# HGRN rounds of a hybrid decoder layer: scores in three groups between products, the first a round ahead, sample dots beside the head squares

## The chip, the cores and the metric

The kernel runs on one core of a Trainium2 chip. The metric is the device time of one execution in microseconds, the median of several runs. Beside it stands one profiled execution, from which all rows come. Round numbers in this text count from 0.

## The reference, cut to what matters

One layer (DEPTH = 1) for a prompt of 512 tokens and a sample group of 8 single tokens that share the weights. The part that the change touches is branch A, the HGRN2 recurrence (8 heads, state 64x64), and the projections that run beside it:

```python
u = xn @ w_in                       # xn: RMSNorm(h), 1024 wide; all branches' columns in one product
f = lb + (1 - lb) * sigmoid(hf)
# HGRN2, chunk by chunk; q = silu(hq), k = 1 - f, v = hi
cum = cumsum(log(f))                                  # within a chunk
o_inter = (q * exp(cum)) @ s
scores[t, s_] = sum_k q[t, k] * exp(cum[t, k] - cum[s_, k]) * k[s_, k]    # s_ <= t
o = o_inter + scores @ v
s_new = exp(last) * s + (k * exp(last - cum)).T @ v
a_hg = head_rmsnorm(o) * silu(hg)
# the 8 sample tokens: one step S = f * S0 + k v^T, o = S^T q, from the given states
# branch B: retention with rotary q and k (rq, rk, rv, rg), then gates ga, gb, output
# projection, ConvFFN (2816 wide), per-layer input embedding, final RMSNorm
```

## The kernel before

Activations lie transposed, channels on the 128 partitions and 520 tokens (512 of the prompt, 8 samples) along the free axis. **Products.** A 128-column tile of weights (128x1024 elements in SBUF) is multiplied with all 520 tokens in two halves of 260. Weights and activations are both split into a high and a low part: ACT copies the loaded tile `raw` into `whi`, rounded (`hi`, line 883), DVE computes `wlo` as the difference (`lo`, line 1250), and PE adds three products for each of 8 channel blocks: 8 x 3 x 2 = 48 matmuls (`product`, line 481, matmuls at line 497). There are two slots of raw, whi and wlo, by the parity of the unit k, and two accumulators `acc`. A slot is refilled when its product is over: ACT and DVE each wait `done(sec, k, it)` for the product's last matmul and then call `ahead(sec, k, it)`, which prepares unit k + 2. All engines run their own program in order; semaphores tie them together.

**Sections.** A and V project the HGRN inputs, B (four rounds) projects rq, rk, rv, rg for retention head `it` and beside it computes HGRN chunk `it` (128 tokens, all 8 heads), C (four rounds) projects the gates and computes retention, D to H are the rest of the layer.

**Scores by levels.** The decayed scores of a chunk of 128 are built in 7 levels: level l covers pairs of neighbouring blocks of 2^l tokens. POOL makes the decayed queries and keys of a level (`first_level` and `next_level`, lines 1700 and 1706; the semaphore `prep` counts them, and level l waits until the scores of level l - 4 have freed its buffer, and for level 3 of the next chunk until `o_ready`). ACT copies the queries with zero padding into `zq[l % 4]` (`pad_queries`, line 950, two ACTIVATE instructions per level; `zq_ready` counts levels). PE computes the scores of a level as fp32 matmuls into a bank of PSUM (`scores(use, it)`, line 615; lines 631 and 635; `sc_full` counts levels). DVE merges a level's bank under a mask into `sfull` (`merge(use, it)`, line 1357, COPY_PREDICATED; `merged` counts). `scores(use, it)` makes the levels 2 use and 2 use + 1 in the two banks of `lvb`; use 3 has level 6 and the eight qk dots per head pair (line 626), which are the diagonal.

**A round on PE (lines 646 to 700), in order:** first half of product 0 (rq); scores 0 (levels 0, 1); second half; scores 1 (levels 2, 3); first half of product 1 (rk); scores 2 (levels 4, 5); second half; scores 3 (qk dots, level 6) and four transposes of the keys into `mb` (659); product 2 (rv); outputs and new state (666, 671, 675); first half of product 3 (rg); head squares (685, 686) and the transposes of rv (581, 583); second half; then the sample dots, 16 small matmuls of the samples' states with `qz` into `mb` (699). `mb` is one bank whose four uses per round are counted by `misc_full` and `misc_free`.

**A round on ACT (993 to 1049):** `vst`; the load of the samples' state `ss`; pad level 4; done product 0, high half of unit 2 (`ahead`), swapped halves `xs`, pads of levels 5 and 6; done product 1, high half of unit 3, xs, `khat`; done product 2, high half of the next round's unit 0, `hiT`; squares `sq`, `sqh`; root `rs`; `vr`, `v8r`; pads of levels 0 to 3 of the next round; done product 3, high half, `ahh`, sigmoid `sg`.

**A round on DVE (1402 to 1456):** merge 0; the gate of the round before; merge 1; done product 0, low half `wlo`, rotary; merge 2; done product 1, low half, kr; merge 3; rotary; sample state; new state `sbd`; `sql`; done product 2, low half; reciprocal of the head norms and gating `ot`; done product 3, low half; copies of the sample dots; `ahl`.

Of the kernel before, what the change touches and what calls it, by code (L numbers as in the profile page):

```python
# [12 lines left out]
NT = 512  # L13
NS = 8
# [6 lines left out]
LV = 7  # L21
# [14 lines left out]
M_B, M_C, M_F, M_G = 3, 19, 35, 36  # L36
# [26 lines left out]
def hybrid_layer(nc, x_prompt, x_sample, state_hgrn, state_ret, state_conv, p_prompt, p_sample,  # L63
# [186 lines left out]
    with ctx:  # L250
        def sem(name):
            return ctx.enter_context(nc.semaphore(name))
# [13 lines left out]
        zq_ready = sem("zq_ready")  # L266
        sc_full = sem("sc_full")
# [99 lines left out]
        def m4(ap):  # L367
            return ap.rearrange("p (a b) -> p a b", a=4)

# [96 lines left out]
        def _(pe):  # L466
            def taken():

                pe.sem_inc(pe_passed, 1)
# [8 lines left out]
            def wait_misc(base, k, it, per):  # L478
                pe.wait_ge(misc_free, it * per + (base + k))
# [135 lines left out]
            def scores(use, it):  # L615


                levels = [l for l in (2 * use, 2 * use + 1) if l < LV]
                pe.wait_ge(zq_ready, it * LV + (levels[-1] + 1))
                pe.wait_ge(merged, it * MERGES + (2 * use + 1))  # L620
                taken()
                if use == 3:
                    for c in range(4):
                        for r in range(2):
                            rows = slice(64 * r, 64 * r + 64)
                            pe.matmul(lvb[rows, 1, 2 * c:2 + 2 * c], qk[:, c, rows], headsel, start=True, stop=True)
                for l in levels:
                    for c in range(4):
                        out = lvb[:, l % 2, c * 128:(c + 1) * 128].rearrange("s (two t) -> s two t", two=2)
# [16 lines left out]
            with pe.Fori(0, 4) as it:  # L646

                def first_scores():
                    pe.wait_ge(v_taken, it * 2 + 9)
                    scores(0, it)  # L650

                halves(0, it, first_scores)
                scores(1, it)
                halves(1, it, lambda: scores(2, it))
                scores(3, it)
                pe.wait_ge(prep, it * 8 + 8)
                wait_misc(M_B, 0, it, 4)
# [11 lines left out]
                wait_misc(M_B, 1, it, 4)  # L669
# [10 lines left out]
                def head_squares():  # L680

                    pe.wait_ge(sq_ready, it + 1)
                    wait_misc(M_B, 2, it, 4)
# [12 lines left out]
                for b in range(NS):  # L696

                    rows = slice(64 * (b % 2), 64 * (b % 2) + 64)
                    mm = pe.matmul(mb[rows, b // 2 * 2:b // 2 * 2 + 2], ss[:, b, :], qz[:, :, b], start=True, stop=True)
                mm.then_inc(misc_full, 1)  # L700
# [173 lines left out]
        def _(act):  # L874
# [118 lines left out]
            def hgrn_chunk(it, last=False):  # L993
                act.wait_ge(misc_full, it * 4 + (M_B - 2))
# [4 lines left out]
                act.wait_ge(misc_full, it * 4 + M_B)  # L999
# [4 lines left out]
                for k, scale in ((0, 1.0), (1, KSCALE)):  # L1004
                    done("B", k, it)
                    ahead("B", k, it)
                    act.wait_ge(rot_done, it * 2 + (k + 1))
                    for a, b in ((0, 64), (64, 0)):
                        act.activation(two(xs[k][a:a + 64, :]), ps2(k, b, b + 64), ACT.Copy,
                                       scale=scale).then_inc(swapped, 1)  # L1010
                    if k == 0:
                        act.wait_ge(vs_stored, 16)
                        for h2 in range(2):
                            v = vs_dram[0, :, bass.ds(it * 128 + 64 * h2, 64)]
                            act.dma_start(vb[64 * h2:64 * h2 + 64, 0:512].rearrange("k (b v) -> k b v", b=NS),
                                          v.unsqueeze(0).broadcast_to([64, NS, 64])).then_inc(vb_loaded, 16)
                        for l in range(5, LV):
                            pad_queries(l, it)
                    else:
                        act.wait_ge(misc_full, it * 4 + (M_B + 1))  # L1020
                        act.activation(khat[:], mb[:], ACT.Copy).then_inc(misc_free, 1)
# [13 lines left out]
                act.wait_ge(misc_full, it * 4 + (M_B + 3))  # L1035
# [202 lines left out]
        def _(dve):  # L1238
# [8 lines left out]
            for first in (*acc_free, rot_done, f_done, merged, o_free, ah_lo, mix_lo, ac_lo, h_new):  # L1247
                dve.sem_inc(first, 1)
# [108 lines left out]
            def merge(use, it):  # L1357

                for n in (2 * use, 2 * use + 1):
# [12 lines left out]
                    src = lvb[:, n % 2, :].rearrange("s (e b h) -> s e b h", e=8, h=hb)  # L1372
# [29 lines left out]
            def hgrn_chunk(it, before=None):  # L1402
# [17 lines left out]
                merge(3, it)  # L1420
# [10 lines left out]
                dve.wait_ge(misc_full, it * 4 + (M_B + 2))  # L1431
# [11 lines left out]
                dve.wait_ge(misc_free, it * 4 + (M_B + 3))  # L1443
# [4 lines left out]
                dve.wait_ge(misc_full, it * 4 + (M_B + 4))  # L1448
                taken()
                own = qT[:, it, NT:TT].rearrange("p (i two) -> p i two", two=2)  # L1450
                dots = mb[:, 0:NS].rearrange("p (i two) -> p i two", two=2)
                for h2 in range(2):
                    for odd in range(2):
                        ins = dve.tensor_copy(own[64 * h2:64 * h2 + 64, :, odd], dots[64 * odd:64 * odd + 64, :, h2])
                ins.then_inc(misc_free, 1)
# [11 lines left out]
            dve.wait_ge(misc_free, M_C)  # L1467
            with dve.Fori(0, 4) as it:
# [215 lines left out]
        def _(pool):  # L1684
# [64 lines left out]
            def hgrn(it, last=False):  # L1749
# [6 lines left out]
                pool.wait_ge(misc_free, it * 4 + M_B)  # L1756
# [145 lines left out]
```

## Time and profile before

| | us |
|---|---|
| median of 3 runs | 919.84 |
| lowest and highest | 919.07, 920.59 |
| the profiled execution | 919.76 |
| its span, first to last instruction | 917.9 |

The page of the profile, cut to the busy digits in 40 slices of 22.9 us each and to the shares of the chain that ended last:

```profile
## 2 busy tenths in 40 slices
PE   9999999999999999999999999999999999999995
...
DVE  6432278888765565665576666666666433435654
ACT  7323446646554555223343333333333222213433
POOL 0006087787111100004621111111111121213431
PEclk9999999999999999999999999999999999999998
```

Each digit is the busy share of a slice in tenths, 9 being 90% or more; PEclk is the granted clock of TensorE in the same tenths. Section B lies in the sixth to the eleventh slice (112 to 247 us). In a timeline row stand the start in us, the time until the last instruction of the row ends, the engine, the line, the operation, what it writes and reads, and the number of instructions; in brackets stands idle time before it and what ended it. PE matmuls overlap in time, so PE's pace is read from starts, not from lengths. One fp32 score matmul is shown with a length of 0.22 us.

### The profile page before, as it was taken

How to read it: one execution, taken by the hardware profiler on the slowest of the kernel's cores; microseconds unless marked ns; L12 is line 12 of the kernel's file. 1: busy time of each engine (PE TensorE's matmuls, PEld its weight loads, DVE VectorE, ACT ScalarE, POOL GpSimd, SP SyncE). 2: the span in 40 equal slices, each digit the busy share in tenths (PEclk: the TensorE clock that was granted, in tenths of full speed). 3: DMA queues.
4: the chain of work that ended last, by engine and by line, in shares of the span. 5: the costliest groups of instructions: out<-in, count | busy, mean ns of one | idle time of the engine just before them, and what ended most of it. 6: DMA issues, size and time to landing. Idle time of an engine off the chain costs nothing.

```text
span 917.9 us, 21087 instructions
## 1 busy us (share of the span) xinstructions
PE 906.6 (99%) x8016; PEld 895.8 (98%) x8016; DVE 533.6 (58%) x651; ACT 370.9 (40%) x511; POOL 238.2 (26%) x289
## 2 busy tenths in 40 slices
PE   9999999999999999999999999999999999999995
PEld 8999999999999999999999999999999999999995
DVE  6432278888765565665576666666666433435654
ACT  7323446646554555223343333333333222213433
POOL 0006087787111100004621111111111121213431
PEclk9999999999999999999999999999999999999998
DMA  7332533233245443633323333333333333332312
GB/s 227 100 93 86 184 94 99 61 92 102 70 129 157 116 130 107 194 119 101 92 70 94 91 91 91 91 91 91 91 91 109 96 94 94 94 92 68 106 34 94
DMA packets 176473, 94.75 MB, mean 103 GB/s; under 512 B 17888, under 2 KB 174960, under 8 KB 176016
## 3 DMA queue, kind: packets, MB, share of 16 engines
q1 hardware_dynamic: 149698, 80.61, 29.5%
q10 hardware_dynamic: 26736, 13.60, 5.4%
q8 instruction: 26, 0.43, 0.2%
q14 instruction: 13, 0.11, 0.0%
HBM read 86.25 MB, written 8.03 MB: 103 GB/s over the span
## 4 chain that ended last, share of the span: by engine, by line
PE 97%; DVE 1%; DMA 1%; ACT 0%; issue 0%; ACTq 0%; SPq 0%; DVEq 0%
PE acc L497 87%; PE lvb L635 1%; DMA xtok<-in_x_prompt 1%; PE lvb L497 1%; PE mb L745 0%; PE ob L671 0%; PE lvb L528 0%; PE lvb L631 0%; PE ob L724 0%; PE mb L728 0%; PE ob L723 0%; PE lvb L709 0%; PE ob L666 0%; PE lvb L581 0%; DVE sfull L1373 0%; PE lvb L833 0%
## 5 line engine op out<-in xcount | busy, mean ns | idle before, releaser
L889 ACT ACTIVATE whi<-raw 128x1024 fp32r<-128x1024 f32 (+2 forms) x132 | 146.8, 1112 | 364.8 <-PE acc L497 363.9
L1254 DVE TENSOR_TENSOR wlo<-raw,whi 128x1024 fp32r<-128x1024 f32 (+2 forms) x131 | 197.7, 1509 | 154.0 <-ACT whi L889 154.0
L497 PE MATMUL acc<-xah,whi 128*128 128x260 f32 x896 | 185.5, 288 | 0.2
L497 PE MATMUL acc<-xah,wlo 128*128 128x260 f32 x896 | 180.3, 283 | 0.0
L497 PE MATMUL acc<-xal,whi 128*128 128x260 f32 x896 | 179.9, 282 | 0.0
L497 PE MATMUL acc<-xbh,whi 128*128 128x260 f32 x816 | 165.0, 283 | 0.0
L497 PE MATMUL acc<-xbh,wlo 128*128 128x260 f32 x816 | 164.4, 283 | 0.0
L497 PE MATMUL acc<-xbl,whi 128*128 128x260 f32 x816 | 164.1, 283 | 0.0
L497 PEld LDWEIGHTS acc<-xah,whi 128*128 128x128 f32 x896 | 137.9, 188 | 2.3
L497 PEld LDWEIGHTS acc<-xah,wlo 128*128 128x128 f32 x896 | 137.9, 188 | 0.0
L497 PEld LDWEIGHTS acc<-xal,whi 128*128 128x128 f32 x896 | 137.9, 188 | 0.0
L497 PEld LDWEIGHTS acc<-xbh,whi 128*128 128x128 f32 x816 | 125.8, 188 | 0.1
L497 PEld LDWEIGHTS acc<-xbh,wlo 128*128 128x128 f32 x816 | 125.8, 188 | 0.0
L497 PEld LDWEIGHTS acc<-xbl,whi 128*128 128x128 f32 x816 | 125.5, 188 | 0.0
L497 PE MATMUL acc<-ach,whi 128*128 128x260 f32 x352 | 71.2, 283 | 0.0
L497 PE MATMUL acc<-ach,wlo 128*128 128x260 f32 x352 | 70.8, 282 | 0.0
L497 PE MATMUL acc<-acl,whi 128*128 128x260 f32 x352 | 70.6, 282 | 0.0
L1798 POOL TENSOR_TENSOR sqt<-hT 128x520 f32 x23 | 36.0, 1567 | 123.3 <-DVE hT L1539 100.8
L1819 POOL TENSOR_TENSOR gg<-gg,cv 128x520 f32<-128x520 f32 x22 | 29.4, 1337 | 116.4 <-DVE gg L1609 113.0
L497 PEld LDWEIGHTS acc<-acl,whi 128*128 128x128 f32 x352 | 54.3, 188 | 0.0
L497 PEld LDWEIGHTS acc<-ach,whi 128*128 128x128 f32 x352 | 54.2, 188 | 0.1
L497 PEld LDWEIGHTS acc<-ach,wlo 128*128 128x128 f32 x352 | 54.2, 188 | 0.0
(307 smaller groups left out, 1172.5 us busy)
## 6 DMA issues: line engine op xcount, KB each, us to landing
raw<-in_w_in SPq DMA_DIRECT2D x96, 256.0 KB, 3.1
raw<-in_w_up SPq DMA_DIRECT2D x88, 256.0 KB, 3.1
raw<-in_w_down SPq DMA_DIRECT2D x16, 384.0 KB, 3.3
raw<-in_w_down SPq DMA_DIRECT2D x16, 320.0 KB, 3.7
raw<-in_w_out SPq DMA_DIRECT2D x16, 256.0 KB, 2.9
raw<-in_w_ple_gate SPq DMA_DIRECT2D x8, 512.0 KB, 3.7
x_transposed<-xstg SPq DMA_DIRECT2D x1, 2080.0 KB, 7.9
hT<-x_transposed ACTq DMA_DIRECT2D x1, 2080.0 KB, 8.8
```

The lines of the kernel that those rows point to most:

```text
L497: mm = pe.matmul(sums[:, b, 0:HT], wt[slot][:, w], xx[:, c, b * HT:(b + 1) * HT], start=first and i == 0 and q == 0, stop=last and i == n ...
L635: mm = pe.matmul(out[64 * r:64 * r + 64, :, 32 * r:32 * r + 32], lk[l % 4][:, c, 64 * r:64 * r + 64], zq[l % 4][:, c, :, 32 * r:32 * r + 3 ...
L889: act.activation(whi[k % 2][:, 0:n], raw[k % 2][:, 0:n], ACT.Copy).then_inc(hi_ready, 1)
L1254: dve.tensor_tensor(wlo[k % 2][:, 0:n], raw[k % 2][:, 0:n], whi[k % 2][:, 0:n].bitcast(fp), SUB).then_inc(lo_ready, 1)
L1798: step(pool.tensor_tensor(sqt[:], hT[:, j, :], hT[:, j, :], MUL))
L1819: pool.tensor_tensor(gg[:], gg[:], cv[:], MUL).then_inc(act_ready, 1)
```

## The change

The levels come in three groups of scores instead of four: levels 0 to 2, 3 to 5, and 6 with the qk dots. They go round three banks, the two of `lvb` and `mb` (`score_bank`). The first group of rounds 1 to 3 is issued at the end of the round before, after product 3; in round 0 it stays in the middle of product 0. The second group stands after product 0, the third after product 1, and both these products are whole. The sample dots leave the round's end: they stand ahead of the head squares in the middle of product 3, write into the free accumulator 0 and are counted by `dots_full` and `dots_free`, so that `mb` has three counted uses a round. ACT pads level 5 right after `ahead("B", 0, it)` and level 6 after the swaps and the DMA issues. DVE merges after `ahead` of product 0 and copies the dots ahead of the reciprocal. PE's program has rounds 0 and 3 written out and a loop over rounds 1 and 2.

```diff
-M_B, M_C, M_F, M_G = 3, 19, 35, 36
+M_B, M_C, M_F, M_G = 3, 15, 31, 32
+        def score_bank(l):
+            return (lvb[:, 0, :], lvb[:, 1, :], mb[:])[l % 3]
             def scores(use, it):
-                levels = [l for l in (2 * use, 2 * use + 1) if l < LV]
+                levels = [l for l in range(3 * use, 3 * use + 3) if l < LV]
                 pe.wait_ge(zq_ready, it * LV + (levels[-1] + 1))
-                pe.wait_ge(merged, it * MERGES + (2 * use + 1))
-                taken()
-                if use == 3:
+                pe.wait_ge(merged, it * MERGES + (3 * use + 1))
+                taken()
+                if use == 0:
+                    pe.wait_ge(v_taken, it * 2 + 9)
+                    wait_misc(M_B, 0, it, 3)
+                if use == 2:
                     ...
-            with pe.Fori(0, 4) as it:
-                def first_scores():
-                    pe.wait_ge(v_taken, it * 2 + 9)
-                    scores(0, it)
-                halves(0, it, first_scores)
+            def hgrn_chunk(it, first=False, last=False):
+                if first:
+                    halves(0, it, lambda: scores(0, it))
+                else:
+                    pe.wait_ge(dots_free, it + 1)
+                    product("B", 0, it, 0, 0, C8, 0, xah, xal)
                 scores(1, it)
-                halves(1, it, lambda: scores(2, it))
-                scores(3, it)
+                product("B", 1, it, 1, 1, C8, 0, xah, xal)
+                scores(2, it)
                 pe.wait_ge(prep, it * 8 + 8)
-                wait_misc(M_B, 0, it, 4)
                 ...
                 def head_squares():
+                    pe.wait_ge(acc_free[0], tidx("B", 2, it) + 1)
+                    pe.wait_ge(smp_staged, it + 1)
+                    pe.wait_ge(ss_ready, it + 1)
+                    taken()
+                    for b in range(NS):
+                        rows = slice(64 * (b % 2), 64 * (b % 2) + 64)
+                        mm = pe.matmul(acc[0][rows, 0, b // 2 * 2:b // 2 * 2 + 2], ss[:, b, :], qz[:, :, b],
+                                       start=True, stop=True)
+                    mm.then_inc(dots_full, 1)
                     pe.wait_ge(sq_ready, it + 1)
                     ...
-                    pe.wait_ge(acc_free[0], tidx("B", 2, it) + 1)
                     v_transposes()
                 halves(3, it, head_squares)
-                wait_misc(M_B, 3, it, 4)
-                pe.wait_ge(smp_staged, it + 1)
-                pe.wait_ge(ss_ready, it + 1)
-                ...
+                if not last:
+                    scores(0, it + 1)
+            pe.sem_inc(dots_full, 1)
+            hgrn_chunk(0, first=True)
+            with pe.Fori(1, 3) as it:
+                hgrn_chunk(it)
+            hgrn_chunk(3, last=True)
+            pe.wait_ge(dots_free, 5)
@@ ACT, hgrn_chunk
-                act.wait_ge(misc_full, it * 4 + M_B)
+                act.wait_ge(dots_full, it + 1)
                 ...
                     done("B", k, it)
                     ahead("B", k, it)
+                    if k == 0:
+                        pad_queries(5, it)
                     act.wait_ge(rot_done, it * 2 + (k + 1))
                     ...
-                        for l in range(5, LV):
-                            pad_queries(l, it)
+                        pad_queries(6, it)
@@ DVE, merge and hgrn_chunk
-                for n in (2 * use, 2 * use + 1):
+                for n in range(3 * use, min(3 * use + 3, LV + 1)):
                     ...
-                    src = lvb[:, n % 2, :].rearrange("s (e b h) -> s e b h", e=8, h=hb)
+                    src = score_bank(n).rearrange("s (e b h) -> s e b h", e=8, h=hb)
                     ...
-                merge(1, it)
                 done("B", 0, it)
                 ahead("B", 0, it)
+                merge(1, it)
                 ...
                 rotate(qr[:, it, :], 0, it)
-                merge(2, it)
                 ...
-                merge(3, it)
+                merge(2, it)
                 rotate(kr[:, it, :], 1, it)
                 ...
                 ahead("B", 2, it)
-                dve.wait_ge(misc_free, it * 4 + (M_B + 3))
-                gate_outputs(ghg, it, 0)
-                done("B", 3, it)
-                ahead("B", 3, it)
-                dve.wait_ge(misc_full, it * 4 + (M_B + 4))
+                dve.wait_ge(dots_full, it + 2)
                 ...
-                ins.then_inc(misc_free, 1)
+                ins.then_inc(dots_free, 1)
+                dve.wait_ge(misc_free, it * 3 + (M_B + 3))
+                gate_outputs(ghg, it, 0)
+                done("B", 3, it)
+                ahead("B", 3, it)
@@ POOL, hgrn
-                pool.wait_ge(misc_free, it * 4 + M_B)
+                pool.wait_ge(dots_free, it + 1)
```

## Rows read from the trace of the kernel before

**Rows 1.** The page: busy time, share of the span, instructions by engine.
```profile
PE 906.6 (99%) x8016; PEld 895.8 (98%) x8016; DVE 533.6 (58%) x651; ACT 370.9 (40%) x511; POOL 238.2 (26%) x289
```

**Rows 2.** Timeline of PE, round 1: first group of scores inside product 0.
```profile
148.84 0.40 PE L497 MATMUL acc<-xah,wlo 128*128 128x260 f32 x2
149.17 1.15 PE L635 MATMUL lvb<-zq,lk 128*64 128x64 f32 x32
150.25 0.51 PE L497 MATMUL acc<-xah,whi 128*128 128x260 f32 x2
150.60 0.40 PE L497 MATMUL acc<-xal,whi 128*128 128x260 f32 x2
150.84 0.40 PE L497 MATMUL acc<-xah,wlo 128*128 128x260 f32 x2
```

**Rows 3.** Timeline of PE: second group of scores after product 0, rounds 1 and 2.
```profile
152.99 0.40 PE L497 MATMUL acc<-xah,wlo 128*128 128x260 f32 x2
153.69 1.15 PE L635 MATMUL lvb<-zq,lk 128*64 128x64 f32 x32 [0.29 <-DVE sfull L1373]
...
186.89 0.40 PE L497 MATMUL acc<-xah,wlo 128*128 128x260 f32 x2
187.40 1.15 PE L635 MATMUL lvb<-zq,lk 128*64 128x64 f32 x32
```

**Rows 4.** Timeline of DVE, round 2: the step ahead of the merges, and a merge.
```profile
183.72 0.69 DVE L1395 TENSOR_TENSOR ahl<-ot,ahh 128x512 f32 x1
...
185.93 1.32 DVE L1373 COPY_PREDICATED sfull<-msk,lvb 128x512 f32<-128x512 uint32 x1 [0.15 <-DVE sfull L1373]
```

**Rows 5.** Timeline of PE: head squares in the middle of product 3, rounds 1 and 3.
```profile
174.94 0.41 PE L497 MATMUL acc<-xah,wlo 128*128 128x260 f32 x2
175.27 0.47 PE L685 MATMUL mb<-sqh,blk64r 128*128 128x512 f32 x1
175.58 0.39 PE L686 MATMUL mb<-sql,blk64r 128*128 128x512 f32 x1
...
242.42 0.41 PE L497 MATMUL acc<-xah,wlo 128*128 128x260 f32 x2
242.67 0.39 PE L685 MATMUL mb<-sqh,blk64r 128*128 128x512 f32 x1
242.90 0.39 PE L686 MATMUL mb<-sql,blk64r 128*128 128x512 f32 x1
```

**Rows 6.** Timeline of PE: sample dots at the end of round 1.
```profile
179.00 0.40 PE L497 MATMUL acc<-xah,wlo 128*128 128x260 f32 x2
179.32 0.63 PE L699 MATMUL mb<-qz,ss 128*64 128x2 f32 x16
180.00 0.51 PE L497 MATMUL acc<-xah,whi 128*128 128x260 f32 x2
```

**Rows 7.** Timeline of PE: last pair of product 1 in round 1; retention scores of section C.
```profile
161.64 0.40 PE L497 MATMUL acc<-xah,wlo 128*128 128x260 f32 x2
...
253.14 1.05 PE L709 MATMUL lvb<-qst,kst 128*128 128x128 f32 x8
```

**Rows 8.** Timeline of ACT: high halves, pads, and the copy ahead of section C's scores.
```profile
162.07 1.06 ACT L889 ACTIVATE whi<-raw 128x1024 fp32r<-128x1024 f32 x1 [2.69 <-PE acc L497]
...
177.26 3.50 ACT L962 ACTIVATE zq<-lq 64x256 f32<-64x256 f32 x8
...
186.66 0.84 ACT L962 ACTIVATE zq<-lq 64x256 f32<-64x256 f32 x2 [1.75 <-POOL tl L1730]
...
252.06 0.62 ACT L1062 ACTIVATE vst<-vr 128x512 f32 x1
```

**Rows 9.** Timeline of POOL, round 1: first and last instruction of levels 4 and 5.
```profile
150.03 0.92 POOL L1726 COPY lq<-lq 128x256 f32<-128x256 f32 x1 [4.52 <-PE lvb L635]
...
154.84 0.22 POOL L1730 TENSOR_TENSOR tl<-tl 128x16 f32<-128x16 f32 x1
```

**Rows 10.** Stretch near the end: us, busy (count) of PE, PEld, DVE, ACT, POOL, granted clock, DMA share, GB/s.
```profile
899.00:908.00 9.00, 8.21 (x71) 8.04 (x71) 3.00 (x5) 4.05 (x7) 2.36 (x2) 1.00 0.01 2
```

More of the change, by code:

```diff
@@ L266, in hybrid_layer @@
         zq_ready = sem("zq_ready")
+        dots_full = sem("dots_full")
+        dots_free = sem("dots_free")
         sc_full = sem("sc_full")
@@ L628, in scores @@
                     for c in range(4):
-                        out = lvb[:, l % 2, c * 128:(c + 1) * 128].rearrange("s (two t) -> s two t", two=2)
+                        out = score_bank(l)[:, c * 128:(c + 1) * 128].rearrange("s (two t) -> s two t", two=2)
                         if l == LV - 1:
@@ L668, in _ @@
                 pe.wait_ge(vst_ready, it + 1)
-                wait_misc(M_B, 1, it, 4)
+                wait_misc(M_B, 1, it, 3)
                 for h in range(8):
@@ L680, in head_squares @@
                 def head_squares():
+                    pe.wait_ge(acc_free[0], tidx("B", 2, it) + 1)
[7 more added lines that the diff above has]
+                    mm.then_inc(dots_full, 1)
                     pe.wait_ge(sq_ready, it + 1)
-                    wait_misc(M_B, 2, it, 4)
+                    wait_misc(M_B, 2, it, 3)
                     pe.wait_ge(sums_ready, 1)
@@ L686, in head_squares @@
                     pe.matmul(mb[:], blk64r[:], sql[:], start=False, stop=True).then_inc(misc_full, 1)
-                    pe.wait_ge(acc_free[0], tidx("B", 2, it) + 1)
                     v_transposes()
                 halves(3, it, head_squares)
-                wait_misc(M_B, 3, it, 4)
-                pe.wait_ge(smp_staged, it + 1)
-                pe.wait_ge(ss_ready, it + 1)
-                taken()
[L696 to L700, printed above, removed]
+                if not last:
[6 more added lines that the diff above has]
+            pe.wait_ge(dots_free, 5)
             pe.wait_ge(v_taken, 17)
@@ L993, in hgrn_chunk @@
             def hgrn_chunk(it, last=False):
-                act.wait_ge(misc_full, it * 4 + (M_B - 2))
+                act.wait_ge(misc_full, it * 3 + (M_B - 1))
                 taken()
@@ L1016, in hgrn_chunk @@
                                           v.unsqueeze(0).broadcast_to([64, NS, 64])).then_inc(vb_loaded, 16)
[L1017 to L1018 removed]
+                        pad_queries(6, it)
                     else:
[L1020 removed]
+                        act.wait_ge(misc_full, it * 3 + (M_B + 1))
                         act.activation(khat[:], mb[:], ACT.Copy).then_inc(misc_free, 1)
@@ L1034, in hgrn_chunk @@
                 act.activation(sqh[:], sq[:], ACT.Copy).then_inc(sq_hi, 1)
-                act.wait_ge(misc_full, it * 4 + (M_B + 3))
+                act.wait_ge(misc_full, it * 3 + (M_B + 3))
                 act.activation(rs[:], mb[:], ACT.Sqrt, bias=eps[:]).then_inc(misc_free, 1)
@@ L1245, in _ @@
             dve.sem_inc(lo_ready, 2)
-            for first in (*acc_free, rot_done, f_done, merged, o_free, ah_lo, mix_lo, ac_lo, h_new):
+            for first in (*acc_free, dots_free, rot_done, f_done, merged, o_free, ah_lo, mix_lo, ac_lo, h_new):
                 dve.sem_inc(first, 1)
@@ L1430, in hgrn_chunk @@
                 dve.wait_ge(prep, it * 8 + 8)
-                dve.wait_ge(misc_full, it * 4 + (M_B + 2))
+                dve.wait_ge(misc_full, it * 3 + (M_B + 2))
                 for h2 in range(2):
@@ L1442, in hgrn_chunk @@
                 ahead("B", 2, it)
-                dve.wait_ge(misc_free, it * 4 + (M_B + 3))
+                dve.wait_ge(dots_full, it + 2)
+                taken()
+                own = qT[:, it, NT:TT].rearrange("p (i two) -> p i two", two=2)
+                dots = acc[0][:, 0, 0:NS].rearrange("p (i two) -> p i two", two=2)
+                for h2 in range(2):
+                    for odd in range(2):
+                        ins = dve.tensor_copy(own[64 * h2:64 * h2 + 64, :, odd], dots[64 * odd:64 * odd + 64, :, h2])
+                ins.then_inc(dots_free, 1)
+                dve.wait_ge(misc_free, it * 3 + (M_B + 3))
                 gate_outputs(ghg, it, 0)
@@ L1447, in hgrn_chunk @@
                 ahead("B", 3, it)
-                dve.wait_ge(misc_full, it * 4 + (M_B + 4))
[L1449 to L1454, printed above, removed]
-                ins.then_inc(misc_free, 1)
                 branch_lo(ahl, ahh, it, 0)
@@ L1467, in _ @@
             dve.wait_ge(misc_free, M_C)
+            dve.wait_ge(dots_free, 5)
             with dve.Fori(0, 4) as it:
```

## The prediction

> **What bounds the kernel now.** I read the page's busy times first. TensorE works 906.6 of 917.9 us [rows 1]; the other engines have a third or more of their time left. So a change to these rounds can only remove or add time between the starts of matmuls, and I read the timeline of PE through one round of section B (round 1: 146.1 to 180.0). After that I read the timelines of ACT, DVE and POOL, to see what each group of small matmuls waits for. A product's matmuls start in pairs every 0.24 us [rows 2]. The sum is made against the profiled execution: 919.76 us, of which 917.9 are span; it lies 0.08 under the median of 919.84, which is nothing. About 0.2% is what a measurement of this kernel can tell from no change.
>
> **Fewer groups of scores.** The two-level group at 149.17 stands in the middle of product 0: 0.33 from the last pair of the product to the group, 1.08 to the next pair, 0.35 to the pair after that [rows 2]. Without it these would be two steps of 0.24, so it costs 1.28. Its row says 1.15 us for 32 matmuls; taking off one matmul's length of 0.22 leaves 0.93 over 31 starts, 0.03 each. The 16 matmuls of a level thus cost 0.48, two levels 0.96, and the remaining 0.32 is the price of breaking into a product. Levels 0 to 5 lie in three groups per round now and in two after: 0.32 x 4 rounds = **-1.28**. The last group (level 6, the qk dots, the four transposes) keeps its content.
>
> **The wait before the second group.** In round 1 the second group starts 0.70 after the last pair, not 0.33, because DVE is still merging; in round 2 it is 0.51 [rows 3], and round 3 is like round 2. Together 0.37 + 0.18 + 0.18 = 0.73. After the change the merges have a whole product to run in. DVE's lateness goes: **-0.73**. The release itself is worth reading: DVE's merge ends at 185.93 + 1.32 = 187.25 [rows 4] and PE starts at 187.40 [rows 3], 0.15 later. I use this 0.15 as the time from a releaser's end to PE's first matmul.
>
> **Sample dots joined to the head squares.** Today the squares start 0.33 after a pair and the second of them 0.31 later in round 1, but 0.25 and 0.23 in round 3 [rows 5]: in rounds 0 to 2 DVE's low half of the squares is slightly late. The dots stand alone at the round's end: 0.33, then 0.68 to the next product [rows 6], then 0.35 as in [rows 2], less the two normal steps (0.48) = 0.88. After, dots come first: 0.33, then 0.68 to the squares (the row's distance to a product; no row has dots ahead of squares, the lowest distance between groups is near nothing, which would be 0.25 less), then 0.23 because DVE is done by then. New minus old in rounds 0 to 2: (0.33 + 0.68 + 0.23) - (0.33 + 0.31) - 0.88 = -0.28; in round 3 (1.24 - 0.48) - 0.88 = -0.12. Sum **-0.96**. The dots' new waits (samples' state, acc 0 free) are met: DVE's state update is over before the head products and ACT frees acc 0 just after product 2. DVE's four copies (0.68) move ahead of its reciprocal and delay the gate by as much, which the next product hides.
>
> **The first group a round ahead.** It now sits between product 3 and product 0, ahead of product 0's waits. After the dots, a group followed by the same waits, the product follows 0.25 after the last small matmul (0.68 less 15 x 0.03), against 0.15 in mid-product (1.08 less 0.93): 0.1 x 3 = **+0.3**. Gains so far: 1.28 + 0.73 + 0.96 - 0.3 = 2.7 us.
>
> **What the second group now waits for.** This decides. Before, the second group needed levels 2 and 3, padded by ACT a round earlier. Now scores(1) asks zq_ready for it*7 + 6, which means six padded levels, 0 to 5, and it comes right after product 0. But ACT pads level 5 only after done("B", 0, it), the end of that same product 0, and after ahead("B", 0, it), the high half of a weight tile. ACT runs in program order, so nothing can bring this pad forward. The chain is counted from the start of the product's last pair: ACT's whi begins 0.43 later (pair at 161.64 [rows 7], whi at 162.07 [rows 8], an ACT that was idle); whi takes 1.06 and the pad 0.84 [rows 8], 0.03 between them; then 0.15 to PE. That is 2.51, where the group would otherwise start at 0.33. The wait is **2.18 us in each of the 4 rounds: +8.7**. Nothing covers it: queued behind the group on PE are product 1 and everything later. POOL isn't the later one: its levels 4 and 5 take 150.03 to 155.06 [rows 9], 5.0 us from the first level's scores, and between these and product 0's end there are some 7 us. DVE isn't either. In round 1's frame its ahl ends at 184.41 [rows 4]; after, the dots have moved but the chain to it is as long; three merges at 1.4 (the slow pace of [rows 4] while POOL works) end at 188.6. The first group starts at about 180.0 (below), product 0 at 180.0 + 47 x 0.03 + 0.25 = 181.7, its last of 24 pairs 0.35 + 22 x 0.24 = 5.6 later at 187.3, and ACT's pad is done at 189.7. DVE has 1.1 us of slack, so the saving of 0.73 holds, but only because the new wait is longer.
>
> **What the first group waits for.** It needs levels 0 to 2 of the next round, and it needs them 3.7 us sooner than before. In round 1 ACT does four pads from 177.26 in 3.50 [rows 8], three of them by 179.89, PE could start at 180.04. PE reaches the place where the dots were at 179.32 [rows 6]; both are tied to the squares, so moving the dots changes nothing in this difference. It is 0.72, three times: **+2.2**. POOL's level 2 is ready over a microsecond before its pad.
>
> **The entry to section C.** ACT's copy vst ends at 252.06 + 0.62 = 252.68 [rows 8], so the retention scores (253.14 [rows 7]) may start at 252.83. ACT's chain is tied to the squares of round 3; PE gets there 0.88 sooner without the dots, at 252.3. **+0.5**.
>
> **The sum.** -2.7 + 8.7 + 2.2 + 0.5 = +8.7 us, rounded once: 919.76 + 8.7 = 928.5 us.
>
> **Bounds.** The wait of the second group is at least whi and pad alone, 1.9 x 4 = 7.6, and at most 2.35 x 4 = 9.4 if ACT takes up the end of product 0 a little later. The first group's wait is 1.8 to 2.7, the entry to C 0 to 0.8, the gains 2.0 to 3.8. Ends: +5.6 and +10.9, 925.4 to 930.7. Unrolling makes three copies of PE's round; sections A and H are unrolled already and PE starts no later there, so I take nothing, and keep 0.5 us on either side for what I don't see.
>
> **Rivals.** (1) Other side: *the padding of level 5 is covered*. Place: scores(1) after product 0. Price: 2.18 a round. It decides from the point at which the pad ends less than 0.33 after the last pair. For it: POOL has level 5 ready early and ACT stands idle before the product's end. Against it: the program order of done, ahead, pad. Then DVE's merges would end last in rounds 1 to 3 (188.75 against 187.6, about 1.1 each, 3.4 together) unless they too run faster. With neither, and with the first group on time as well, all gains are kept: 919.76 - 2.7 = 917.1. Chance 3%.
> (2) *The padding is covered but the first group's wait, the entry to C and perhaps some merges remain*: 919.76 - 2.7 + 2.2 + 0.5 = 919.8, up to 923 with the merges. Chance 4%, most of it within 0.2%.
> (3) *The clock falls in the new waits.* The granted clock is 1.00 even in the stretch with the longest pause of the trace, in which PE is busy 8.21 of 9.00 us [rows 10]; that stretch has one wait of about 1 us, and none here lasts 2.2. If TensorE fell from 2.4 to 1.2 GHz at each second group and stayed there for product 1, its 24 pairs (5.8 us) would take twice as long: 5.8 x 4 = 23 us, so 952. Chance 3%.
> The Trainium skill ("TensorE: Matmul & The Clock Gate", "The HAM clock gate") says that an idle array is throttled to half its clock and only activity lifts it; by that rule a wait can cost more than its own length. The trace has no wait of 2 us within dense work, so it doesn't show which way this goes.
>
> **Chances.** The forecast (both new waits, clock unchanged): 90%. Rivals 3, 4 and 3%. Faster by over 0.2% 0.03; within 0.2% 0.04; slower by over 0.2% 0.93. The range 925.0 to 931.5 leaves out the rivals and takes in the bounds.
>
> **What would show it.** In the changed profile, the idle time of PE before line 635's second group should be 2.2 us in each round with ACT's zq as its releaser, and ACT's timeline should read whi, then zq, then PE's start 0.15 later. The first group should start 0.15 after ACT's sixth pad of the series of eight. The squares should show 0.23 between them in all rounds. Products 0 and 1 should be 48 matmuls without a break. If the group after product 0 starts without an idle stretch, my reading of the count on zq_ready is wrong and the change is a small gain; if product 1 shows pairs at 0.48, the clock has fallen.

## The result

The changed kernel takes 932.71 us, median of 4 runs (931.73 to 934.93), against 919.58 (919.07 to 920.59) for the kernel before: ratio 1.0141, 95% interval 1.0129 to 1.0153. That is 13.1 us slower; the forecast was 8.7 us slower with a range up to 931.5. The profiled execution is 932.80 us with a span of 931.0, 13.0 more than before; the readings below account for these 13.0.

Each run also has its mean granted clock. Of the four, 0.990 goes with 932.80, 0.992 with 931.73 and 932.62, 0.988 with 934.93; the profiled execution of the kernel before had 0.996.

### The profile page after: what moved, and what is told of

The parts are those of the page before. It is cut to its first block, busy times and chain, and to the rows that moved or that the text cites. A ratio compares the mean times of both kernels' runs of the same rounds, so it can differ in the third digit from the quotient of the medians.

```text
span 931.0 us, 21039 instructions
## 1 busy us (share of the span) xinstructions
PE 908.6 (98%) x8016; PEld 898.7 (97%) x8016; DVE 536.5 (58%) x651; ACT 370.3 (40%) x511; POOL 240.0 (26%) x289
## 4 chain that ended last, share of the span: by engine, by line
PE 94%; DVE 1%; issue 1%; ACT 1%; ACTq 1%; POOL 0%; DVEq 0%; POOLq 0%
PE acc L502 84%; PE lvb L644 1%; PE lvb L502 1%; ACT zq L979 1%; PE acc L514 1%; PE mb L644 0%; PE mb L762 0%; PE ob L679 0%; PE lvb L726 0%; PE lvb L640 0%; PE mb L745 0%; PE ob L741 0%; PE ob L674 0%; PE ob L740 0%; ACTq L1034 0%
```

## The profile after

The timeline of PE in the changed kernel around the wait before the second group of scores, rounds 0 and 1 (start in us, length, engine, line, operation, count; idle time before it and what ended it in brackets). Line 502 is the products' line (497 before), 644 the scores' (635 before), 979 the pads' (962 before).

```profile
119.16 0.40 PE L502 MATMUL acc<-xah,wlo 128*128 128x260 f32 x2
121.61 1.15 PE L644 MATMUL lvb<-zq,lk 128*64 128x64 f32 x32 [2.05 <-ACT zq L979]
122.56 0.67 PE L644 MATMUL mb<-zq,lk 128*64 128x64 f32 x16
123.15 0.51 PE L502 MATMUL acc<-xah,whi 128*128 128x260 f32 x2
...
155.19 0.40 PE L502 MATMUL acc<-xah,wlo 128*128 128x260 f32 x2
157.73 1.84 PE L644 MATMUL lvb<-zq,lk 128*64 128x64 f32 x32 [2.14 <-ACT zq L979]
159.31 1.12 PE L644 MATMUL mb<-zq,lk 128*64 128x64 f32 x16
160.36 0.80 PE L502 MATMUL acc<-xah,whi 128*128 128x260 f32 x2
160.96 0.58 PE L502 MATMUL acc<-xal,whi 128*128 128x260 f32 x2
161.38 0.40 PE L502 MATMUL acc<-xah,wlo 128*128 128x260 f32 x2
```

Two things are to be read. From the last pair of product 0 to the second group there are 2.45 us in round 0 and 2.54 in round 1, where [rows 2] has 0.33: the wait is there, it is ended by the pad, and it is 2.12 and 2.21 long. And the same group of 48 small matmuls takes 1.54 to the next product in round 0, but 2.63 in round 1; the next pairs follow at 0.60 and 0.42 instead of 0.35 and 0.24. That is 1.09 + 0.25 + 0.18 = 1.52 us lost without any wait. Rounds 2 and 3 show the same (1.5 each), behind waits of 2.21 and 2.04.

ACT beside the wait of round 1: the high half of the next tile, then the pad, and PE starts 0.24 after the pad's end (also in round 2; in rounds 0 and 3, which PE's program has written out, it is 0.15).

```profile
155.71 1.06 ACT L906 ACTIVATE whi<-raw 128x1024 fp32r<-128x1024 f32 x1 [1.77 <-PE acc L502]
...
156.67 0.82 ACT L979 ACTIVATE zq<-lq 64x256 f32<-64x256 f32 x2
```

The same places as stretches, in the changed kernel: us, busy time (count) of PE, PEld, DVE, ACT, POOL, granted clock, DMA share, GB/s. The first is the wait of round 0, the others follow the waits of rounds 1 and 3.

```profile
119.30:121.70 2.40, 0.35 (x6) 0.17 (x6) 1.11 (x2) 1.99 (x4) 2.16 (x6) 1.00 0.01 3
157.70:161.20 3.50, 3.47 (x52) 3.38 (x53) 2.68 (x4) 1.84 (x4) 3.11 (x8) 0.53 0.67 168
233.00:236.50 3.50, 3.44 (x51) 3.36 (x52) 2.61 (x4) 1.96 (x4) 3.04 (x7) 0.51 0.68 169
```

The granted clock is the last but two: TensorE ran at 1.2 GHz, half of its 2.4, for nearly all of the 3.5 us after these waits, and at 1.00 before them and during the waits themselves (155.20 to 157.70 in round 1).

The first group of scores, at the end of round 0, and the squares of round 1 in the changed kernel (PE), with the pads that release the first group (ACT):

```profile
146.72 0.40 PE L502 MATMUL acc<-xah,wlo 128*128 128x260 f32 x2
148.03 1.15 PE L644 MATMUL lvb<-zq,lk 128*64 128x64 f32 x32 [0.91 <-ACT zq L979]
...
179.73 0.41 PE L502 MATMUL acc<-xah,wlo 128*128 128x260 f32 x2
180.07 0.63 PE L698 MATMUL acc<-qz,ss 128*64 128x2 f32 x16
180.63 0.50 PE L704 MATMUL mb<-sqh,blk64r 128*128 128x512 f32 x1
180.97 0.39 PE L705 MATMUL mb<-sql,blk64r 128*128 128x512 f32 x1
```

```profile
145.10 3.50 ACT L979 ACTIVATE zq<-lq 64x256 f32<-64x256 f32 x8
```

From the last pair to the first group there are 1.31 us instead of 0.33, a wait of 0.98. Six of the eight ACTIVATE instructions are over at 145.10 + 2.63 = 147.73, and PE starts 0.30 later, not 0.15. At the ends of rounds 1 and 2, inside PE's loop, the waits are 1.03 and 1.06, and PE starts 0.47 and 0.50 after the sixth ACTIVATE. The dots and the squares are 0.34, 0.56 and 0.34 apart.

The entry to section C (line 726 is 709 before):

```profile
265.41 0.40 PE L502 MATMUL acc<-xah,wlo 128*128 128x260 f32 x2
266.13 1.04 PE L726 MATMUL lvb<-qst,kst 128*128 128x128 f32 x7 [0.32 <-ACT vst L1080]
```

0.72 instead of 0.24: 0.48 us of waiting for ACT's copy.

The sum over the profiled executions, from distances between starts of matmuls:

| term | forecast | measured |
|---|---|---|
| work and waits saved in section B | -2.7 | -2.9 |
| wait before the second group, 4 rounds | +8.7 | +8.6 |
| wait before the first group, 3 times | +2.2 | +3.1 |
| entry to section C | +0.5 | +0.5 |
| half clock after three of the waits | 0 | +4.4 |
| before section B | 0 | -0.7 |
| sum | +8.7 | +13.0 |

The last term but one sums the 1.52, 1.46 and 1.47 us of rounds 1 to 3. The -0.7 before section B is not counted to the change. It lies in the first 112 us, where both kernels issue the same matmuls, and the profiles of other kernels that differ from the changed one only behind that point have their first scores anywhere from 114.86 to 117.44 us, against 114.87 here and 115.53 before. Part of it shows near the start: the pair of 128-column matmuls at 8.58 us of the kernel before (line 509) lasts 0.64 us, the same pair at 8.06 us of the changed kernel (line 514) only 0.39.

## The experiments

Two questions were open: is the wait for level 5's pad really the main cause, and does the clock's fall come from this wait, from both waits together, or from the new order of the work? A third: is there anything in the change that costs by itself (whole products, a third bank, the joined dots), and what is left of it without the waits?

**The change once more, for the clock.** No edit.

> The changed kernel again, unchanged, for a second trace beside the next run. Theory (a wait of about 2.2 us before the second group may let the clock fall, by chance of where in time it lies): again 2 to 4 stretches of half clock of 3.4 us, each right at the end of such a wait, but not always in the same rounds; 932 to 935 us. Rival (something fixed in rounds 1 to 3 makes it fall): exactly those three again.

Measured: 933.69 us (before on the same chip 920.46; 1.0150, interval 1.0133 to 1.0167). The trace shows the half clock after the same three waits, rounds 1 to 3, and not after round 0's. The mean clocks of its four runs are 0.990, 0.988, 0.990 and 0.988, with 933.1, 934.3, 933.1 and 934.7 us. One stretch of 3.4 us at half clock lowers the mean of 931 us by 0.0018, so these runs differ by about one such stretch, which goes with 1.2 to 1.6 us. It need not lie in section B: the kernel before, whose profile has no fall there, shows the same step on this chip (0.994 with its three longest times, 920.7 to 920.9 us, and 0.995 or 0.996 with the others, 919.3 to 920.5). The rounds are more regular than expected: two traces have the same three rounds, as the rival said. So whether the falls of section B come by chance isn't settled by these two.

```profile
158.20:161.60 3.40, 3.40 (x50) 3.28 (x46) 2.68 (x5) 1.49 (x4) 2.85 (x9) 0.50 0.72 183
```

This stretch of 3.4 us in round 1 is wholly at half clock.

**Half of the wait filled with work.** Run beside the previous one on the same chip. After product 0:

```diff
+                pe.wait_ge(o_free, it + 1)
+                for _ in range(4):
+                    pe.matmul(ob[:, 0:128], ones128[:], ones1024[:], start=True, stop=True)
                 scores(1, it)
```

> The changed kernel with 4 fp32 products (8 matmul records, 0.89 us) in the wait before the second group in all rounds; results not used. PE then idles about 1.2 us there instead of 2.1, at the same total time. Theory (idleness of about 1 us doesn't make the clock fall, as the waits of 1.0 us before the first group don't): no fall, 928.5 us, like the version with 1.77 us of work. Rival (any wait in this place can do it): falls in some rounds and 930 to 933 us.

Measured: 928.77 us, 1.0096 (1.0079 to 1.0113), mean clock 0.994 to 0.996. Timeline of PE and the stretch after the wait, round 1 (line 664 is the added work):

```profile
155.25 0.40 PE L502 MATMUL acc<-xah,wlo 128*128 128x260 f32 x2
155.48 1.05 PE L664 MATMUL ob<-ones,ones 128*128 128x128 f32 x8
157.79 1.15 PE L644 MATMUL lvb<-zq,lk 128*64 128x64 f32 x32 [1.25 <-ACT zq L982]
158.74 0.67 PE L644 MATMUL mb<-zq,lk 128*64 128x64 f32 x16
159.34 0.51 PE L502 MATMUL acc<-xah,whi 128*128 128x260 f32 x2
```

```profile
157.70:161.20 3.50, 3.41 (x63) 3.37 (x64) 3.00 (x5) 1.91 (x4) 3.25 (x8) 1.00 0.64 161
```

The second group starts 2.54 after the last pair, exactly as in the changed kernel, so the wait is unchanged; only PE's idleness in it is cut to 1.25. The clock stays at 1.00, the group takes 1.55 again, and the kernel gains 4.9 us on the previous run. Between the first scores of round 0 and the qk dots of round 3 the two profiles differ by 4.5 us (122.78 against 127.30). That is the cleanest evidence of the study: useless work made the kernel faster. It gives the price of the falls, and with the wait unchanged and only PE's idleness cut, no fall came; idle times of 0.91 to 1.28 us, of which this trace has seven, were followed by none.

**More of the wait filled.** As before with `range(8)`, and an earlier version with `range(16)`.

> The changed kernel with 8 fp32 products (16 matmul records of 0.11 us, 1.77 us) into the free output bank between product 0 and the second group, in all four rounds; their results are not used. The longer version had 32 records (3.46 us) and so stood out of the wait by 1.4 us a round. Now the padding ends after them, and they should add nothing. Theory (the fall of the clock comes from PE's idleness in this wait and costs 4.4 us): no fall in section B, waits otherwise as in the changed kernel, 932.7 - 4.4 = 928.3 us, which is the forecast made without a fall. Rival (the fall costs less than read from starts, other things filled the difference): 930 or more.

Measured: 929.20 us, 1.0098 (1.0083 to 1.0113), no fall in section B. Expected 928.3; filling more than half brings nothing further.

> The changed kernel with 16 fp32 matmuls of 128 columns into the free output bank between product 0 and the second group, in rounds 1 to 3 (their results are not used). At 0.11 us each they take 1.8 of the 2.1 us for which PE waits there, so they add nothing. Theory (PE's idleness in this wait makes the clock fall, and the fall costs 4.4 us in three rounds): the clock stays at 1.00 in section B and the time is 932.7 - 4.4 = 928.3, close to the forecast without a fall. Rival (the clock falls for another reason, or its fall costs nothing): 932.7.

Measured: 934.54 us, 1.0161. A miss of mine in the sizing: each fp32 matmul stands as two records of 0.11 us, so 16 of them last 3.46 us and not 1.8. The edit also puts them into all four rounds, not into rounds 1 to 3 as the expectation says.

```profile
157.37 0.40 PE L502 MATMUL acc<-xah,wlo 128*128 128x260 f32 x2
157.61 3.73 PE L664 MATMUL ob<-ones,ones 128*128 128x128 f32 x32
161.27 0.92 PE L644 MATMUL lvb<-zq,lk 128*64 128x64 f32 x24
```

3.90 from the pair to the group instead of 2.5 is 1.4 too long in each of four rounds; 932.7 + 5.6 - 4.4 = 933.9, near the time measured. Here too the clock stayed at 1.00.

**The wait alone, in the kernel before.** Groups, banks and cut products as before; only ACT pads level 3 late, and level 4 behind it:

```diff
 # ACT, pads ahead of round 0
-                        for l in (2 * k, 2 * k + 1):
+                        for l in (0, 1) if k == 0 else (2,):
                             pad_queries(l, 0)
 ...
-                pad_queries(4, it)
                 for k, scale in ((0, 1.0), (1, KSCALE)):
                     done("B", k, it)
                     ahead("B", k, it)
+                    if k == 0:
+                        pad_queries(3, it)
+                        pad_queries(4, it)
                     ...
-                    for l in range(4):
+                    for l in range(3):
                         pad_queries(l, it + 1)
```

> The kernel before, with ACT padding level 3 only after product 0 and the high half of the next tile (level 4 behind it). Products are cut and groups placed as before; only this wait is added. Theory (a wait for whi and one pad costs 2.2 us in each of 4 rounds wherever it stands, less the 0.7 that DVE's merges cost there already): 919.6 + 8.0 = 927.6 if the clock stays, 932 if each wait of rounds 1 to 3 also lets it fall for a stretch. Rival (uncut products or the third bank are what costs time): about 920. Which of 927.6 and 932 comes tells whether this wait alone lets the clock fall, or only together with the waits before the first group, which this kernel hasn't.

Measured: 932.49 us, 1.0140 (1.0123 to 1.0157), the same as the whole change. PE in round 1, and the stretch behind the wait:

```profile
155.13 0.40 PE L497 MATMUL acc<-xah,wlo 128*128 128x260 f32 x2
157.67 1.97 PE L635 MATMUL lvb<-zq,lk 128*64 128x64 f32 x32 [2.14 <-ACT zq L962]
159.57 0.80 PE L497 MATMUL acc<-xah,whi 128*128 128x260 f32 x2
```

```profile
157.60:161.10 3.50, 3.43 (x39) 3.35 (x40) 1.92 (x3) 2.72 (x6) 2.14 (x5) 0.52 0.32 74
```

This decides two points. The wait for one high half and one pad is worth what was summed, wherever it stands. And it alone lets the clock fall; the waits before the first group, which this kernel doesn't have, aren't needed for it. Again the fall comes in rounds 1 to 3 and not in round 0, where PE idles 2.14 us as in rounds 1 and 2.

**The first group back in product 0, all rounds.**

```diff
-                if first:
-                    halves(0, it, lambda: scores(0, it))
-                else:
-                    pe.wait_ge(dots_free, it + 1)
-                    product("B", 0, it, 0, 0, C8, 0, xah, xal)
+                pe.wait_ge(dots_free, it + 1)
+                halves(0, it, lambda: scores(0, it))
                 ...
-                if not last:
-                    scores(0, it + 1)
```

> The changed kernel with the first group of scores back in the middle of product 0 in all four rounds, still three levels and three banks. Theory: the waits before the first group (1.0 us each in rounds 1 to 3) go, the waits before the second group stay: 932.7 - 3.1 = 929.6 if the clock falls as before, 925.2 if it needs both waits close together. Rival (the first group a round ahead is worth something by itself): 933 or more.

Measured: 929.40 us, 1.0110 (1.0093 to 1.0127). The 3.1 us of the first group's waits are real and go away. The number hides a trade, though: in the profiled execution the second group waits longer, 2.9 us from product to group in round 1, because POOL starts level 4 only after the first group's scores, and the half clock shows in two rounds instead of three.

```profile
154.55 0.40 PE L502 MATMUL acc<-xah,wlo 128*128 128x260 f32 x2
157.44 0.77 PE L644 MATMUL lvb<-zq,lk 128*64 128x64 f32 x19 [2.50 <-ACT zq L973]
```

This wait of 2.50 us was not followed by a fall, while waits of 2.14 were. Its length alone doesn't decide. In rounds 2 and 3 of this trace the idle times are 2.44 and 2.24 and the clock falls; in round 3 not at once, for the first 32 small matmuls still take 0.95 to the next ones, and only the 16 after them take 1.03 instead of 0.59.

**Level 5 padded before product 0 ends.**

```diff
                 pad_queries(4, it)
+                pad_queries(5, it)
                 for k, scale in ((0, 1.0), (1, KSCALE)):
                     done("B", k, it)
                     ahead("B", k, it)
-                    if k == 0:
-                        pad_queries(5, it)
```

> The changed kernel, with ACT padding level 5 right after level 4, before it waits for product 0. Theory (the second group waits for a pad that ACT may only start after product 0, and these long waits let the clock fall): the waits of 2.1 to 2.2 us before the second group go (8.6 together), DVE's third merge ends last instead in rounds 1 to 3 (about 0.4 each), and the clock stays at 1.00 through section B (4.4 more): 932.7 - 8.6 + 1.2 - 4.4 = 921 us. Rival (the clock falls for the waits before the first group, or for the new order of work, whatever the second group waits for): the clock still falls, and 925 us.

Measured: 925.21 us, 1.0058 (1.0041 to 1.0075): 7.5 better than the change, but 4 short of the expectation. The profiled execution is the slowest of the four (928.1; the others 924.7 to 925.5), and the excess lies ahead of section B, whose first scores start at 117.44 us instead of 114.87. The clock stays at 1.00 through section B. What is left is read from ACT, POOL and DVE in round 1:

```profile
157.82 0.84 ACT L979 ACTIVATE zq<-lq 64x256 f32<-64x256 f32 x2 [1.49 <-POOL tl L1747]
```

```profile
152.39 1.61 POOL L1745 TENSOR_TENSOR lq<-lq,tl 128x256 f32<-128x256 f32 x1
...
156.22 0.63 POOL L1745 TENSOR_TENSOR lq<-lq,tl 128x256 f32<-128x256 f32 x1
```

```profile
152.17 1.34 DVE L1271 TENSOR_TENSOR wlo<-raw,whi 128x1024 fp32r<-128x1024 f32 x1 [0.34 <-ACT whi L906]
153.43 1.13 DVE L1412 TENSOR_TENSOR ahl<-ot,ahh 128x512 fp32r<-128x512 f32 x1
```

The pad is no longer behind ACT's tile but behind POOL, whose levels 4 and 5 now take 151.27 to 157.62 = 6.3 us, not the 5.0 of [rows 9]. One and the same multiply takes 0.63 in level 5 and 1.61 in level 4; beside level 4 DVE splits a tile and takes the difference `ahl`. The group stands 1.90, 0.99, 0.90 and 0.83 us later than without a wait in the four rounds, 4.6 together where the expectation had 1.2: that is most of the miss. The Trainium skill ("GPSIMD Engine Reference", "1. Specifications") says that POOL shares its SBUF interfaces with VectorE and that DVE instructions with two SBUF inputs contend; both DVE operations here have two, and the row agrees. That it is this port and nothing else no run here isolates.

**The joined dots alone.** The kernel before with the dots ahead of the squares, in accumulator 0, and their copies ahead of the reciprocal; all else as before.

> The kernel before with one part of the change alone: the sample dots ahead of the head squares, in accumulator 0. Groups, banks, pads and cut products as before. Theory: the part is a gain, as summed in the prediction: -1.0 us, 919.4 - 1.0 = 918.4. Rival (the dots are late for their state or the earlier copies on DVE push the gate into a wait): 919.4 or more. Section C's first scores wait 0.5 us for ACT in either case, which is in neither number: with it 918.9.

Measured: 919.78 us against 919.74, 1.0003 (0.9994 to 1.0012): no gain that can be told, and none of 1.0. On PE the joined part does nearly what was summed: from round 2's first scores to round 3's there are 33.52 us in this kernel and 33.73 before, 0.21 less where the sum has 0.28. But most of it is given back in two places, the 0.5 at the entry to section C, and the merges of round 1:

```profile
152.52 0.40 PE L502 MATMUL acc<-xah,wlo 128*128 128x260 f32 x2
153.46 0.74 PE L643 MATMUL lvb<-zq,lk 128*64 128x64 f32 x18 [0.55 <-DVE sfull L1382]
```

0.94 here, 0.70 in [rows 3]: PE arrives earlier, and DVE, whose copies now stand ahead of the reciprocal, doesn't. The two places make 0.7 of the 1.0; the rest is less than these runs can tell.

**Groups that ask only for pads in reach.** The changed kernel with three groups of other levels:

```diff
+GROUPS = ((0, 1), (2, 3, 4), (5, 6, 7))
 def scores(use, it):
-    levels = [l for l in range(3 * use, 3 * use + 3) if l < LV]
+    levels = [l for l in GROUPS[use] if l < LV]
-    pe.wait_ge(merged, it * MERGES + (3 * use + 1))
+    pe.wait_ge(merged, it * MERGES + (1, 3, 6)[use])
 ...
-    mm = pe.transpose(mb[:, c * 128:(c + 1) * 128], lk[3][:, c, :], ident)
+    mm = pe.transpose(ob[:, c * 128:(c + 1) * 128], lk[3][:, c, :], ident)
 # DVE, end of a round
     gate_outputs(ghg, it, 0)
+    if not last:
+        merge(0, it + 1)
     done("B", 3, it)
     ahead("B", 3, it)
```

> The changed kernel with the same number of groups (three), but levels 0 and 1 in the first, a round ahead, 2 to 4 in the second, 5, 6 and the qk dots in the third, so that each group asks only for levels that ACT has padded before the product in front of it ends; the key transposes go into the output bank, which is free then, and DVE merges the first group before it splits the next weight tile. Theory (the only costs of the change are the two waits for pads and the fall of the clock): both waits shrink to under 0.3 us, the clock stays, and the part of the change that saves work between products is left: 916.7 to 918 us, below the kernel before. Rival (whole products or a third bank cost something by themselves): 919.4 or more.

Two more parts of the edit are left out above: PE asks for the pads last, behind the waits on `v_taken`, `mb` and `merged`, and ACT reads `khat` from the output bank.

Measured: 917.29 us against 919.74 (ratio 0.9969, 0.9957 to 0.9981), faster than both kernels. Both waits are gone; PE at the end of round 0 and after product 0 of round 1:

```profile
145.01 0.40 PE L503 MATMUL acc<-xah,wlo 128*128 128x260 f32 x2
145.40 1.15 PE L645 MATMUL lvb<-zq,lk 128*64 128x64 f32 x32
...
152.12 0.40 PE L503 MATMUL acc<-xah,wlo 128*128 128x260 f32 x2
152.44 0.69 PE L645 MATMUL mb<-zq,lk 128*64 128x64 f32 x16
152.96 1.10 PE L645 MATMUL lvb<-zq,lk 128*64 128x64 f32 x32
```

0.39 and 0.32 from pair to group; the longest of the seven is 0.48, in round 0. With the same number of groups, whole products, three banks and joined dots, what remains is a gain of 2.5 us, near the 2.7 of the sum's first parts less 0.4 at the entry to C, where PE still waits. So nothing else in the change costs more than these runs can tell (the interval of the gain is 1.7 to 4.0 us).

## Why the prediction was right and wrong

**Right: the direction and the main term.** The wait before the second group was forecast from program order alone (the count on `zq_ready`, and ACT's done, ahead, pad) and its length from three rows: 2.18, measured 2.12, 2.21, 2.21 and 2.04. The late-pad run in the kernel before shows it by itself. The parts of the length agree less well than their sum: in round 1 ACT's tile begins 0.52 after the last pair and not 0.43, and PE starts 0.24 after the pad and not 0.15, while tile, gap and pad together take 1.78 and not 1.93. That these nearly cancel is luck. *Fewer groups*, *the wait of the merges*, *sample dots* and *the entry to section C* came out within 0.2 us in sum. In the sample dots the split was wrong and the sum right: 0.34 + 0.56 + 0.34 is 1.24, as forecast, but the squares stay 0.34 apart in all rounds, also when DVE isn't late. So the 0.31 of [rows 5] was not DVE's lateness. PE's program could have told: it waits for `sq_ready` once, ahead of both squares, so a late DVE can't part them. What sets the distance wasn't tried.

**Wrong: the rival on the clock.** It was named, with 3%, and priced as a whole product at half speed (23 us). The measured fall lies between that and nothing: about 3.4 us at half clock after the waits of rounds 1 to 3, 1.5 us each, 4.4 together (4.9 by the half-filled wait). The step that failed is the term that isn't in the sum: the clock was taken as unchanged through the new waits, at a cost of nothing, on the granted clock of [rows 10]. That stretch has one idle time of 0.79 us. In the profiles of section B none of the 29 idle times of up to 1.28 us that a pad ended was followed by a fall, but 11 of the 16 between 1.97 and 2.50 were (the changed kernel twice, the late pad in the kernel before, the first group back in product 0). The evidence didn't reach as far as the forecast needed it, and 3% was far too little for a rule that spoke for a fall and a trace that said nothing. Without the falls the kernel takes 928.8 to 929.2 us by the two filled waits, inside the range. The Trainium skill ("TensorE: Matmul & The Clock Gate", "The HAM clock gate") has an idle array throttled to half its clock; the granted clock of 0.51 to 0.53 after three waits agrees, the 1.00 after round 0's wait of the same length shows that not every such wait does it.

**Mis-sized: what the first group waits for.** 2.2 forecast, 3.1 measured. The release costs 0.30, 0.47 and 0.50 from the pad's end and not 0.15, which makes 0.8 of the missing 0.9. Behind the pad's wait PE's program has three more waits here, on `merged`, `v_taken` and `mb`, which are met but, I take it, still stepped through. The 0.15 of [rows 4] was read at a wait that is the last one. The second group, with one wait behind the pad's, agrees: 0.15 where the round is written out, 0.24 in the loop. No run takes these waits away, so this cause is read from the rows and the program and not shown by itself. The rest is ACT's first pad, which begins 0.1 later after round 0's squares than after round 1's, which I had taken for all.

**Half right: "POOL isn't the later one".** POOL's levels 4 and 5 run from 148.89 to 155.22 in round 1 of the changed kernel, and product 0's last pair ends at 155.19 + 0.40 = 155.59: it held by 0.4 us and not by the 2 us that I gave it.

```profile
155.01 0.21 POOL L1748 TENSOR_TENSOR tl<-tl 128x16 f32<-128x16 f32 x1
```

The length of POOL's levels was taken from a place in which DVE did other things; a round ahead they fall beside DVE's splitting and take 6.3 us. It did no harm to the sum, since ACT's pad starts only at 156.67, but it made the prices of the first two rivals wrong: with the padding covered, POOL ends last, not DVE, and the run with the early pad came out at 925, not at 920 to 923.

**Right for the change, wrong alone: "which the next product hides".** DVE's copies ahead of the reciprocal cost nothing in the changed kernel, whose second group waits longer: DVE's merges end at 155.77 in round 1 and the group starts at 157.73. In the kernel before they lengthen a merge wait by 0.24.

## What to carry to other kernels

When work is regrouped between the products of a full TensorE, write down for each new group the last thing it asks for and where the producing engine does it in its own program order; here one count on a semaphore reached past an instruction that could only run after the product in front. Then don't price a new wait on TensorE at its length alone; here most waits from 1.97 us on cost more. Look for the longest pause in the trace at which the clock is known to hold, and treat anything beyond it as open, not as safe. If such a wait can't be avoided, a little useless work in it can pay.

## What was not expected of the hardware

- A single idle time of TensorE of 1.97 to 2.15 us between dense products was followed by about 3.4 us at 1.2 GHz in three of four rounds, in the changed kernel twice traced and in the kernel before with the late pad; idle times of up to 1.3 us never were, nor the one of 1.8 in the run with the early pad. In the run with the first group back in product 0, those of 2.24 and 2.44 us were and those of 2.05 and 2.50 weren't. What decides between falling and not, and why round 0 was spared each time, stays open.
- The cost of one such stretch was 1.5 us, less than half of its length. It begins with small matmuls, and these lost less than half: the group of 48 went from 1.54 to 2.63, where twice the time would be 3.08.
- The time from the releaser's end to PE's first matmul was 0.15 us where the deciding wait is the last one (kernel before), 0.15 (written out) and 0.24 (in the loop) with one met wait behind it, and 0.30 (written out), 0.47 and 0.50 (in the loop) with three. That the met waits are the reason is inferred.
- The same POOL multiply of 128x256 took 1.61 us beside two DVE operations with two SBUF inputs and 0.63 beside merges.
